# The last feed-forward block's up product by Strassen's seven half-block products, with two small edits in the first block

## The reference, cut to what matters

```
for i in range(DEPTH):                      # first block, two layers
    mods = sc @ ada_w[i] + ada_b[i]         # 6 * 1024 modulations per layer
    cmods = scc @ ada_w[i] + ada_b[i]
    ...
    h = rms_norm(x, n1) * (1 + sc1) + sh1
    ... split_proj(h @ w_in) ...
...
h = rmsnorm(x, ln2[l])                      # second block, its end
gate = causal_dwconv(h @ w_gate[l], ffn_conv[l])        # three taps
x = x + (jax.nn.silu(gate) * (h @ w_up[l])) @ w_down[l]
return rmsnorm(x, ln_f)
```

## Time and profile before

| | us |
|---|---|
| median of three runs | 2676.16 (2674.49 to 2676.9) |
| the profiled execution | 2671.5, of which the span is 2669.7 |
| PE busy in the span | 2496.6 (94%) |
| DVE, ACT, POOL busy | 1294.1, 988.8, 410.4 |

### The profile page before, as it was taken

One profiled execution on the slowest core, in us unless ns is written; L12 is line 12 of the kernel. 1 busy time (PEld: TensorE's weight loads), 2 busy tenths in 40 slices (PEclk: granted clock), 3 DMA queues, 4 the chain that ended last, 5 costly groups with the idle time before them and its releaser, 6 DMA issues.

```text
span 2669.7 us, 35435 instructions
## 1 busy us (share of the span) xinstructions
PE 2496.6 (94%) x13920; PEld 1523.5 (57%) x13920; DVE 1294.1 (48%) x2490; ACT 988.8 (37%) x1879; POOL 410.4 (15%) x281
## 2 busy tenths in 40 slices
PE   6998998899999999797969999999899998999998
PEld 4875566433333333686754434343677887788886
DVE  3596445344444445586442333333766654442342
ACT  5215553234444443626523222222443333322222
POOL 0222102001110111134100000000324311122221
PEclk9999999899999999999989999999999998999999
DMA  6215724689999998420039999999122011222221
GB/s 274 73 48 221 270 78 168 253 322 382 386 388 385 386 384 349 147 79 17 33 134 386 421 421 421 421 421 406 57 89 80 17 32 48 89 93 99 91 87 56
DMA packets 85509, 567.91 MB, mean 213 GB/s; under 512 B 11640, under 2 KB 12024, under 8 KB 20320
## 3 DMA queue, kind: packets, MB, share of 16 engines
q1 hardware_dynamic: 79944, 550.27, 52.4%
q0 software_dynamic: 3616, 11.80, 1.9%
q10 hardware_dynamic: 1784, 3.58, 0.4%
HBM read 550.92 MB, written 14.68 MB: 212 GB/s over the span
## 4 chain that ended last, share of the span: by engine, by line
PE 47%; DVE 3%; ACT 1%; DMA 1%; issue 1%; POOL 0%; DVEq 0%; ACTq 0%
PE PS L1121 12%; PE PS L1238 4%; PE PS L1236 4%; PE PS L1237 4%; PE PS L1250 3%; PE PS L1252 3%; PE PS L1251 3%; PE PS L1195 2%; PE PS L1226 2%; PE PS L861 1%; DMA RF<-in_w_down_dram 1%; PE PS L1368 1%; PE PS L1268 1%; PE PS L1373 1%; PE PS L1282 1%
## 5 line engine op out<-in xcount | busy, mean ns | idle before, releaser
L2867 POOL TENSOR_TENSOR WHL<-RING,WHL 128x1024 fp32r<-128x1024 f32 x65 | 175.7, 2703 | 849.9 <-ACT WHL L1498 849.9
L1236 PE MATMUL PS<-RR,WHL 128*128 128x512 f32 x512 | 205.8, 402 | 1.8 <-DVE RR L2594 1.8
L1498 ACT ACTIVATE WHL<-RING 128x1024 fp32r<-128x1024 f32 x131 | 136.5, 1047 | 191.2 <-PE PS L1252 119.5
L1238 PE MATMUL PS<-RR,WHL 128*128 128x512 f32 x512 | 203.7, 398 | 0.0
L1237 PE MATMUL PS<-RR,WHL 128*128 128x512 f32 x512 | 202.0, 395 | 0.0
L1121 PE MATMUL PS<-RING,RF 128*64 128x512 f32 x816 | 185.8, 599 | 0.7 <-issue 0.7
L1121 PE MATMUL PS<-WIDE,RF 128*64 128x512 f32 x792 | 182.0, 596 | 0.0
L2065 DVE TENSOR_TENSOR WHL<-RING,WHL 128x1024 fp32r<-128x1024 f32 x66 | 82.8, 1256 | 142.4 <-ACT WHL L1498 139.5
L1791 ACT ACTIVATE RF<-PS,MODS,MSC 128x128 f32<-128x128 f32 x192 | 73.1, 444 | 180.4 <-PE PS L1195 128.7
L1121 PE MATMUL PS<-RF 128*64 128x512 f32 x544 | 127.5, 596 | 0.5 <-DMA RF<-in_w_down_dram 0.5
L1121 PE MATMUL PS<-X,RF 128*64 128x512 f32 x528 | 124.0, 601 | 0.4 <-DMA X<-in_w_down_dram 0.4
(11 more groups left out here) (414 smaller groups left out, 5175.6 us busy)
## 6 DMA issues: line engine op xcount, KB each, us to landing
RING<-in_w_gate_dram SPq DMA_DIRECT2D x61, 1024.0 KB, 8.7
WIDE<-in_w_down_dram SPq DMA_DIRECT2D x52, 1024.0 KB, 11.7
RING<-in_ada_w_dram SPq DMA_DIRECT2D x44, 1024.0 KB, 6.3
RING<-in_w_up_dram SPq DMA_DIRECT2D x42, 1024.0 KB, 9.6
X<-in_w_gate_dram SPq DMA_DIRECT2D x38, 1024.0 KB, 11.1
AR<-in_w_up_dram SPq DMA_DIRECT2D x37, 1024.0 KB, 9.9
RF<-in_w_down_dram SPq DMA_DIRECT2D x31, 1024.0 KB, 13.6
RING<-in_w_in_dram SPq DMA_DIRECT2D x30, 1024.0 KB, 5.0
```

The source lines that it names most:

```text
L1236: e.matmul(o, h[:, j, :], HTH2[:, j, :], start=j == 0, stop=False)
L1238: ins = e.matmul(o, lo[:, j, :], HTH2[:, j, :], start=False, stop=j == 7)
L1498: e.activation(h, load_buffer(ld)[:, js, cs], ACT.Copy).then_inc(act, A(("hi", st["i"])))
L2867: e.tensor_tensor(lo, load_buffer(loads[st["load"]])[:, js, cs], h.bitcast(F32), ALU.subtract).then_inc(pool, G(("lo", st["i"])))
```

## The change

Four things change.

1. **Up product by seven products.** The feed-forward goes in units of two column tiles. For each unit the up product (1024 by 256 weights with 1024 by 512 hidden values) is made in Winograd's form of Strassen's scheme: seven products of a 512x128 weight block with a 512x256 block of hidden values, each 4 blocks times 3 matmuls of 256 columns. Four of the weight operands are sums, made by POOL in float32 (`SUMS`, in the tail of `X`); four of the operands of the hidden values are sums too, made once before the first unit by POOL and DVE from a float32 copy `XF`, then split by ACT and DVE. DVE puts the results together with six additions, some on two quarters at once, and multiplies once for the two tiles.
2. **The feed-forward in three parts** of 8, 8 and 6 tiles, with the down product after each. The load ring there has three buffers. `WHL` is handed out in six halves: a product takes one, a gate or down step takes two. Which engine makes a low part follows `low` for gate and up, and the look-ahead follows the buffers.
3. **Paired first tiles.** In `project` the first two tiles of the order are made together, block by block.
4. **Modulations transposed.** PE transposes `ROW4` in four steps and DVE adds the four row groups by a `tensor_reduce`, then the bias.

```diff
-FFN = ((0, 1536), (1536, 2816))
+FFN = ((0, 8), (8, 16), (16, 22))
+SEVEN = (1, 2, 6, 5, 7, 3, 4)
+    for part, (t0, t1) in enumerate(FFN):
+        for u in range(t0 // 2, t1 // 2):
+            plan += [("w",), ("gate", 2 * u), ("sum", u, 1), ("sum", u, 2), ("conv", 2 * u)]
+            if u == 0:
+                plan += [("other",), ("operand", 6), ("operand", 5)]
+            plan += [("silu", 2 * u), ("w",), ("gate", 2 * u + 1), ("sum", u, 3), ("sum", u, 4), ("conv", 2 * u + 1)]
+            if u == 0:
+                plan += [("operand", 7), ("operand", 4)]
+            for p in SEVEN:
+                plan += [("w",), ("product", u, p)]
+                plan += {1: [("E", u)], 2: [("silu", 2 * u + 1)], 6: [("U2", u), ("C11", u)], 7: [("UB", u), ("C22", u)],
+                         4: [("UC", u), ("gu", u)]}.get(p, [])
+            plan += [("gh", u), ("gl", u)]
+        plan += [("down", part, 0), ("down", part, 1)]
...
+                sums = dict(enumerate({1: 0, 2: 0, 4: 0, 5: 1, 6: 2, 7: 3, 3: 4}[p] for p in SEVEN))
...
+                          single=mode == "u", low=mode == "u" and m in (1, 6) or mode == "f" and cc % 256 == 128)
...
-            q = (q + 1) % NQ
-            st.update(q=q, after=wide, before=last_q.get(q), pool=nq % 2 == 1)
+            q = (q if st["single"] else q + q % 2) % (2 * NQ)
+            mine = (q,) if st["single"] else (q, q + 1)
+            st.update(q=q, after=wide, before=max((last_q[h] for h in mine if h in last_q), key=lambda b: b["i"], default=None),
+                      pool=st["low"] if "unit" in ld or ld["name"] == "w_gate2" else nq % 2 == 1)
...
-        while done < len(steps) and done <= used + LOOK:
+        while done < len(steps) and (done <= used + LOOK if done < ffn else steps[done]["before"]["i"] < used):
...
-    return loads, steps, ahead
+    n = len(ahead) - (len(steps) - ffn)
+    return loads, steps, ahead, ahead[:n] + [[]] + ahead[n:-1]
...
-                    for c in range(4):
-                        ins = e.matmul(o[:, 2 * c:2 * c + 2], ROW4[:, 128 * c:128 * c + 128], SEL[:, 0:2], start=True, stop=True)
-                    ins.then_inc(pe, P(("adat", l, u)))
+                    turned(o, 128, [ROW4[:, 128 * c:128 * c + 128] for c in range(4)], ("adat", l, u))
...
+                for some in (order[:2], *([one] for one in order[2:])):
...
                     for j in range(8):
+                        for (f, s, t0, n), o in zip(some, outs):
...
+                            e.matmul(o, h[:, j, :], HTH[:, j, z], start=j == 0, stop=False)
+                            e.matmul(o, h[:, j, :], HTL[:, j, z], start=False, stop=False)
+                            ins = e.matmul(o, lo[:, j, :], HTH[:, j, z], start=False, stop=j == 7)
...
+                    for j in range(4):
+                        e.matmul(o, h[:, j, :], xh[:, j, :], start=j == 0, stop=False)
+                        e.matmul(o, h[:, j, :], xl[:, j, :], start=False, stop=False)
+                        ins = e.matmul(o, lo[:, j, :], xh[:, j, :], start=False, stop=j == 3)
...
+            for j in range(2, 8):
+                e.wait_ge(dve, V["x3T", j])
+                e.activation(XF[:, j, :], held("x3T", j), ACT.Copy, scale=VEC[:, V_LN2 + j:V_LN2 + j + 1]).then_inc(act, A(("xf", j)))
             preload(ACT.Silu, 504)
...
-                b4 = held("adat", l, u)[:, 0:8].rearrange("p (c s) -> p c s", s=2)
-                e.tensor_tensor(m_, b4, VEC[:, qv:qv + 4].unsqueeze(2).to_broadcast([128, 4, 2]), ALU.add
+                b4 = held("adat", l, u).rearrange("p (c i r) -> p c r i", i=4, r=32)[:, :, 0:2, :]
+                e.tensor_reduce(m_, b4, AX.X, ALU.add).then_inc(dve, V())
+                e.wait_ge(dve, V.n)
+                e.tensor_tensor(m_, m_, VEC[:, qv:qv + 4].unsqueeze(2).to_broadcast([128, 4, 2]), ALU.add
...
+                elif what == "other":
+                    e.wait_ge(pool, G["other", 6])
+                    e.wait_ge(act, A["xf", 7])
+                    e.tensor_tensor(TQ[7], R22, R12, ALU.subtract).then_inc(dve, V(("other", 7)))
+                    e.tensor_tensor(TQ[4], R21, TQ[6], ALU.subtract).then_inc(dve, V(("other", 4)))
+                elif what == "operand":
+                    p, = k
+                    e.wait_ge(act, A["operand", p])
+                    e.tensor_tensor(OPERAND[p][1], TQ[p], OPERAND[p][0].bitcast(F32), ALU.subtract).then_inc(dve, V(("operand", p)))
...
+                    e.tensor_tensor(GS[u % 3], Q[:, 0:1024], GS[u % 3], ALU.mult).then_inc(dve, V(("gu", u)))
...
+            e.wait_ge(act, A["xf", 3])
+            e.wait_ge(pool, G["xf", 1])
+            e.tensor_tensor(TQ[5], R12, R11, ALU.subtract).then_inc(pool, G(("other", 5)))
+            e.wait_ge(act, A["xf", 7])
+            e.wait_ge(pool, G["other", 5])
+            e.tensor_tensor(TQ[6], R22, TQ[5], ALU.subtract).then_inc(pool, G(("other", 6)))
...
+                    if i in (2, 4):
+                        e.wait_ge(pool, G["sum", u, i // 2])
+                    e.tensor_tensor(o, a, c, op).then_inc(pool, G(("sum", u, i)))
```

More of the change, by code:

```diff
@@ L121, in add @@
                 parts = [((slice(j, j + 2), slice(0, cw)), k0 + j, 2, 0) for j in range(0, nj, 2)]
-            for part, kk, n, cc in parts:
-                st = dict(i=len(steps), load=len(loads) - 1, raw=mode == "raw", part=part, k0=kk, n=n, c0=cc)
+            for m, (part, kk, n, cc) in enumerate(parts):
+                st = dict(i=len(steps), load=len(loads) - 1, raw=mode == "raw", part=part, k0=kk, n=n, c0=cc, sum=sums.get(m, 0),
+                          single=mode == "u", low=mode == "u" and m in (1, 6) or mode == "f" and cc % 256 == 128)
                 ld["steps"].append(st)
@@ L177, in weight_steps @@
             add("w_out2", (), k0, 4, half, 512, "k")
[L178 to L181, removed]
+    last_block, ffn = len(loads), len(steps)
+    for t0, t1 in FFN:
+        for u in range(t0 // 2, t1 // 2):
+            add("w_gate2", (), 0, 8, 256 * u, 256, "f")
+            add("w_up2", (), 0, 8, 256 * u, 256, "u")
+            loads[-1]["unit"] = u
         for half in (0, 512):
-            add("w_down2", (), r0, (r1 - r0) // 128, half, 512, "k")
-    for ld in loads[third:]:
-        ld["slots"] = (0, 1, 2, 3)
+            add("w_down2", (), 128 * t0, t1 - t0, half, 512, "k")
+    for n, ld in enumerate(loads[third:]):
+        ld["slots"] = (0, 1, 2, 3) if n < last_block - third else (0, 1, 2)
     for st in steps[mix:mix + LOOK + 1]:
@@ L816, in sync @@
                             e.wait_ge(dve, V["lo", st["i"]])
+                    if "unit" in ld["before"]:
+                        e.wait_ge(pool, G["sum", ld["before"]["unit"], 4])
                 if "fresh" in ld:
@@ L905, in project @@
                     order[1], order[2] = order[2], order[1]
[L906 to L912, removed]
-                    for j in range(8):
[L914 to L919, removed]
-                        e.matmul(o, h[:, j, :], HTH[:, j, z], start=j == 0, stop=False)
-                        e.matmul(o, h[:, j, :], HTL[:, j, z], start=False, stop=False)
-                        ins = e.matmul(o, lo[:, j, :], HTH[:, j, z], start=False, stop=j == 7)
-                    if s == parts[-1][0]:
-                        ins.then_inc(pe, P(("pf", l, f, s), ("w", st["i"])))
-                    else:
-                        ins.then_inc(pe, P(("pf", l, f, s)))
@@ L2047, in scalar @@
-                if pairs[-1][0] == FFN[part][1] // 128 - 1:
-                    nf = (FFN[part][1] - r0) // 128
-                    for half in range(2):
-                        tokens(nf)
+                elif what == "gh":
+                    u, = k
+                    part = next(n for n, (t0, t1) in enumerate(FFN) if 2 * u < t1)
+                    fl = 2 * u - FFN[part][0]
+                    e.wait_ge(dve, V["gu", u])
+                    if part and fl == 0:
+                        e.wait_ge(pe, P["down2", part - 1, 1, 3])
+                    e.activation(GH[:, fl:fl + 2, :], GS[u % 3].rearrange("p (a b) -> p a b", a=2), ACT.Copy).then_inc(act, A(("gh", u)))
@@ L2832, in vector @@
             split2(HTH2, HTL2, "x3T", V_LN2)
[L2833 to L2835 removed]
+            for what, *k in plan3:
+                if what == "w":
                     weights()
[L2837 removed]
+                elif what == "down":
+                    part, half = k
+                    tokens(("down2", part, half), FFN[part][1] - FFN[part][0], True, "2d" if part + 1 == len(FFN) else None, VECY)
+                elif what == "conv":
+                    f, = k
+                    g_ = GS[f // 2 % 3][:, 512 * (f % 2):512 * (f % 2) + 512]
```

241 lines of the change are left out of this document (172 added, 69 removed).

## The result

The change makes the kernel slower: 2684.23 us median (2680.89 to 2687.06) against 2675.64 us, ratio 1.003 with a 95% interval of 1.0021 to 1.0039, so +8.6 us. The forecast was 2671.2 and the range ended at 2683.

What follows compares the result with a forecast made beforehand. PE, busy for all 350 us of the last feed-forward, was taken as the bound. Terms +1.9 (feed-forward) - 4.4 - 0.3 - 0.2 - 2.0 = -5.0 us, off the median 2676.16, gave 2671.2; range 2662 to 2683.

Steps and rivals of the forecast that it cites:

- The small edits: Paired first tiles in layers 1 and 0 (-4.4, -0.3 us) and transposed modulations (-0.2, -2.0 us), outside the feed-forward.
- Up product: Feed-forward: 84 matmuls of 256 columns replace 48 of 512, 1.1 us less in each of 11 units, -12.3 us.
- Rival 3: Up product: 256-column matmuls are paced by their weight loads, +65 us; chance 3%.
- Stall in every unit: Each unit but the first: PE waits 0.4 us for the third product's low part behind DVE's convolution, +4.3 us.
- Second down step: After parts one and two, its low part comes after the last `gl` on DVE, +0.4 us.
- First unit: Feed-forward start: DVE's list and POOL's sums on the shared port make PE wait, +8.5 us, bounds 6.2 and 12.
- every turn about: First unit's upper bound: POOL and DVE alternate on the shared port, 12 us.
- Clock: First unit: PE's idleness lowers its granted clock for the following 256-column work, +1.0 us, bounds 0 and 3.
- A third part: Feed-forward: eight extra DVE additions of 0.7 lie beside 5.6 us down steps and cost nothing.
- Paired tiles: First two tiles of a layer: pairing keeps PE busy, -4.4 us in layer 1 and -0.3 in layer 0.
- Modulations: 4 transposes replace 8 matmuls, DVE gains a reduction: -0.2 us at the start, -2.0 among the heads.
- the second: Feed-forward rival: POOL's port use delays the next gate tile's low part on DVE, 2684.7 us; chance 15%.

Runs made afterwards that it cites:

- e6_third: Changed kernel with DVE splitting the third and fourth product's weights ahead of the second gate tile's convolution in every unit; 2674.37 against 2676.56 us before.
- e8_all: Changed kernel with early sums, reordered first unit, early low parts in other units, and down step's low part ahead of `gl`; 2661.26 against 2676.56 us before.
- e10_pool_waits: Changed kernel, DVE's order kept, POOL starting a down step's low part only after DVE made the previous step's; 2676.74 against 2675.65 us before.
- e5_sums: Changed kernel with POOL making the first unit's four up-weight sums during the last mixing steps; 2679.57 against 2676.56 us before.
- e7_first: Changed kernel with early sums and DVE's and ACT's first-unit order set by PE's need, convolution of tile 1 last; 2677.52 against 2676.56 us before.
- e9_late_conv: e8_all with the next gate tile's low part before gate tile 1's convolution in the first unit, that tile's Silu later; 2661.28 against 2675.65 us before.

## Why the prediction was wrong, point by point

The small edits came out as forecast, within the noise. The feed-forward is +14.4 where I had +1.9, and three terms make the 12.5 us: the second down step 7.7 (3.2 of it slow matmuls), the first unit with its clock 2.7, the stall in every unit 2.1.

- **Up product, -12.3: right.** 84 matmuls take 10.07 to 10.08 us where nothing waits (e6_third, e8_all). Rival 3, pacing by weight loads, didn't happen.
- **Stall in every unit, +4.3: mechanism right, size short.** It measured 0.64 to 0.65 a unit, +6.4 (e6_third takes it away). There are two waits, 0.29 and 0.15, and after each the next matmul comes 0.10 late. I had seen the first wait only.
- **Second down step, +0.4: the step that failed, without a warning.** The chain that I added up on DVE was right to 0.05 us (e10_pool_waits: 0.25). What I left out is the overlap: POOL's low part of the third step holds the port when DVE comes, though I had used just this mechanism for the first unit. It cost 2 x 2.4 us of waiting, and behind both waits slow matmuls for 1.6 us each: +8.1 in all.
- **First unit, +8.5: the wrong value between right bounds.** I let DVE, once it had the port, run its list in one row. The trace has them alternate: POOL started at 2302.94, 2304.96, 2307.17 and 2309.37, each inside one of DVE's, and each of DVE's four operations of 1.2 took about 2.25. My upper bound, "every turn about", was 12. By the distance of starts the waits came to 8.7 and 0.9, and the unit to 12.2 us over its 21.3, of which 2.2 are clock. The early sums (e5_sums) show that the alternation is worth 4.3 us of the wait before product 1, of which 1.5 come back in the products. The new order took another 4.6 away (e7_first), and with the later convolution 3.4 of the 12.2 are left (e9_late_conv). In that rest PE's two longest waits besides that for the first block, 1.2 and 0.6, are for low parts that POOL makes.
- **Clock, +1.0: too small.** 24 matmuls of 0.213 in place of 0.120 after the long wait (2.2 us), 1.6 after each of the two down waits: 5.4 us, contained in the terms above. I had looked for it in one place, since I saw only one long wait.
- **A third part, 0: right.** Without waits the first two down stages take 44.97 us for 192 matmuls each (0.234 a matmul), and the third shows none either, though DVE adds eight times more.
- **Paired tiles, -4.7: mechanism right, size smaller in most traces.** The median gives -3.7 with an interval that can't tell. The stretch measured 11.29 as forecast in two traces of nine and 12.7 to 12.8 in seven, where slow matmuls follow the wait at its start; I had put that clock at nothing in layer 1. The later start of 0.7 us was missed too. The two tiles save 3.7 us in the one case and 2.0 to 2.2 in the other.
- **Modulations, -2.2: right within the measurement,** -2.9.

The small edits gave -6.4 to -6.6 where I had -6.9, each of these figures known to some 4 us. The rival that came nearest is the second, 2684.7: seven products pile up on DVE. Its time fits the result, its place doesn't. The next gate tile's low part was never late in after, a unit took 21.92 us and not over 22.4, and the loss sat in the first unit and at the down stages.

## What to carry over

When a port or an engine is shared, write down the list of both engines around every point where the bottleneck could wait, also where one chain alone seems to make it in time: here POOL came 0.14 us ahead of DVE, and putting it behind gave PE back 3.7 us in each of two down stages. Two full queues on the port took every turn about in the first unit, and elsewhere DVE held POOL off for several operations, so work out both: each operation at the sum of both until one list is empty, and one list ahead of the other. Work that doesn't depend on the late input, as the sums of the weights, belongs ahead of the handover, and a low part belongs ahead of work that nobody waits for.

## What the runs showed of the hardware that was not expected

- **Two orders on the shared port.** In the first unit neither engine kept the port for more than one instruction: five of DVE's took 10.6 us in after, 6.3 with one POOL operation beside them. It is no rule. In layer 1 of the same trace DVE did hold POOL off, as in the earlier trace rows. POOL and DVE, start and duration:

```profile
1132.37 6.09 POOL L2984 TENSOR_TENSOR WHL<-RING,WHL 128x1024 fp32r<-128x1024 f32 x1 [8.29 <-ACT WHL L1562]
...
1129.57 6.62 DVE L2230 SCALAR_TENSOR_TENSOR AR<-AR,VEC 128x501 f32<-128x501 f32 x10
```

  DVE's ten run at 0.73 us each, six of them in part or whole beside POOL's operation, which ends 2.3 us after the last of them. What decides between the two orders no run here shows.
- **The same wait has two prices.** PE idles 2.27 us before the second down step in after and in e5_sums. In after its next matmuls start 0.43 us apart and the stage takes 49.01; in e5_sums they start 0.23 apart and the stage takes 47.47. e7_first and e8_all differ in the same way behind one and the same wait of 2.3 us, first e8_all, then e7_first, PE in order of time:

```profile
2315.88 0.80 PE L1280 MATMUL PS<-RR,WHL 128*128 128x512 f32 x1 [2.29 <-DVE WHL L2159]
2316.47 0.63 PE L1281 MATMUL PS<-RR,WHL 128*128 128x512 f32 x1
2316.90 0.63 PE L1282 MATMUL PS<-RR,WHL 128*128 128x512 f32 x1
```

```profile
2313.94 0.50 PE L1280 MATMUL PS<-RR,WHL 128*128 128x512 f32 x1 [2.28 <-DVE WHL L2159]
2314.28 0.39 PE L1281 MATMUL PS<-RR,WHL 128*128 128x512 f32 x1
2314.51 0.40 PE L1282 MATMUL PS<-RR,WHL 128*128 128x512 f32 x1
```

  The starts are 0.43 apart in the one (1.2 GHz) and 0.23 in the other (2.4 GHz), at places 1.9 us apart in their spans. Which level follows a wait of this length stays open; its price was 0 or 1.5 us here. The wait of about 2.1 to 2.4 us before the paired tiles of layer 1 is a third such place: nothing in two traces, 1.4 to 1.5 us in seven.
- **A wait costs more than its length at the higher level too:** the matmul behind the one that waited comes 0.10 us late, which made 0.2 us of the 0.64 in each unit.
